# Retention in a two-block forward pass: plain products split into halves, squares summed on the Pool, wider value weights

## The chip, the core and the metric

The kernel runs on one core of one Trainium2 chip. The metric is the device time of one execution in microseconds, lower is better. One launch computes a whole forward pass over 512 tokens of width 1024 through several mixers and feed-forward layers, all of it in 32-bit floats.

## What is computed

The change touches one mixer, the retention of the second block ("odd"). Cut from the reference:

```python
def retention(q, k, v):                    # 4 heads, dk = 256, dv = 512
    ...
    dmask = jnp.where(diff >= 0, jnp.exp(lg[:, None, None] * jnp.maximum(diff, 0.0)), 0.0)
    ...
    def step(state, inp):
        qi, ki, vi = inp
        a = jnp.einsum('bhjd,bhmd->bhjm', qi, ki) * dmask
        o = jnp.einsum('bhjm,bhme->bhje', a, vi) + jnp.einsum('bhjd,bhde->bhje', qi, state) * xi
        state = state * g_chunk + jnp.einsum('bhmd,bhme->bhde', ki * zeta, vi)
        return state, o

def odd_mixer(h, w_in, out_norm, w_out, pos):
    z = h @ w_in
    q = rope(z[..., :nq].reshape(B, S, RET_HEADS, RET_QK), pos)
    k = rope(z[..., nq:2 * nq].reshape(B, S, RET_HEADS, RET_QK), pos)
    v = z[..., 2 * nq:2 * nq + nv].reshape(B, S, RET_HEADS, RET_V)
    g = z[..., 2 * nq + nv:]
    o = rmsnorm(retention(q, k, v), out_norm)
    o = o.reshape(B, S, nv).astype(h.dtype) * jax.nn.silu(g)
    return o @ w_out
```

## The kernel before

**Layout.** Activations lie transposed: 128 features in the partitions, 512 tokens along the row. The kernel needs no chunks: for each head it forms all causal scores of 512 x 512 tokens in four row blocks `j` of 128 key tokens, and block `j` needs only the queries from `j * 128` on, so its rows are 512, 384, 256 and 128 columns wide. `dec` holds the decay by distance.

**Products of halves.** A float product with a weight is made of three products on rounded halves. A value is split in `hi`, the value rounded to the type fp32r, and `lo`, the residual `value - hi`, which is rounded to fp32r too. `mm3` then adds `hi*hi`, `lo*hi` and `hi*lo` in one PSUM bank. ScalarE makes `hi` (a copy), VectorE makes `lo` (a subtraction). Some products are left plain: both operands are ordinary floats in `arena`, and the trace shows two MATMUL records for each of them. In the rows, `split` is the same memory as `arena`, seen as fp32r.

**Weights.** SyncE loads units of 2048 columns (1 MB) in turn into three buffers `wraw`; `W.round(act, name)` makes `whi` and `W.rest(dve, name)` makes `wlo`, in two buffers each. Both calls go up to one unit ahead of the unit named, and a unit's `whi` can't be written before TensorE is done with the unit two places earlier. So in the order of a head, the unit behind the one in use gets ready while that one is multiplied, provided that ScalarE and VectorE come to it in time. TensorE waits for a unit with `W.ready(name)`, which is VectorE's event.

**Order within a head** (`tensor` of `odd`): queries and keys (`u_qk`, two units of 256 columns, 4 blocks of 24 products of 512 columns, `x` moving); values (`u_v`, two units of 256 columns of weights, 8 blocks of 24 products of 256 columns, the weights moving beside 128 tokens of `x`); scores (8 plain products); gates (`u_g`, as queries); weighted values `o` (4 blocks of 4 plain products), with the squares of the block before summed by a plain product with `ones` (`sum_squares`) in between; then the output projection of the head before (`outs[hd - 1]`, 8 blocks of 12 products). The last head's projection follows at the end. `fm_tensor`, `tm_tensor` and `add_tensor` issue these blocks. Each engine runs its own list in the order written, and waits on counters of the others.

**Beside it.** ScalarE copies queries, keys and values out of PSUM (`raw`, `vt`), applies Silu to the gates, squares `o`, and after the fourth sum makes the root (table load, Ln, Exp: `rstd_scalar`) and the `hi` of the gated values. VectorE rotates queries and keys (12 operations into `qk`, waiting for the copy of all four blocks), multiplies the scores by `dec` into `pts`, and after the root gates each of four tiles (`stt` and `tt`), forms `lo` and, in between, adds the projection of the head before to the residual stream `h`. The gating of head `hd` so stands behind its own `o`, while TensorE does the projection of head `hd - 1`. The Pool fetches `dec` for each head and is otherwise free in this stage.

Of the kernel before, what the change touches and what calls it, by code (L numbers as in the profile page):

```python
# [11 lines left out]
P = 128  # L12
# [373 lines left out]
def build(nc, D, phases):  # L386
    ctx = ExitStack()
    with ctx:
# [2669 lines left out]
        def odd(ends, prev, nxt):  # L3058

            S = Stage("retention", sem)  # L3060
# [4 lines left out]
            raw = al(2048)  # L3065
            oo = [[als() for _ in range(4)] for _ in range(2)]
            cos, cos_src, l_c = con("cosq", "odd")
            sin, sin_src, l_s = con("sinq", "odd")
            qk, vt, pts, gg = (al(2048) for _ in range(4))
            tmp, rs, ot = al(T), al(T), [al(T), al(T)]  # L3070
            dec = al(512)
            l_dec = landing("dec")
            u_qk = [fm_units(f"qk{hd}", 512, [(Wi[:, hd * 256:hd * 256 + 256], 0), (Wi[:, 1024 + hd * 256:1280 + hd * 256], 256)])
                    for hd in range(4)]
            u_v = [tm_units(f"v{hd}", Wi, 2048 + hd * 512, 512, 4) for hd in range(4)]
# [3 lines left out]
            def tensor(pe):  # L3079
                for hd in range(4):  # L3080
                    for _ in fm_tensor(pe, S, u_qk[hd], X8, norm.made, fresh=None if hd else norm):
                        pass
                    for _ in tm_tensor(pe, S, u_v[hd], X8, norm.made):
                        pass
                    for j in range(4):
                        nt = T - j * P
                        b = ps.take("s", hd, j)
                        pe.wait_ge(S.V.of("roped", hd), ps.empty("s", hd, j))
                        for d in range(2):
                            i_ = pe.mm(b[:, 0:nt], qk[:, (2 + d) * T + j * P:(2 + d) * T + (j + 1) * P],  # L3090
                                       qk[:, d * T + j * P:(d + 1) * T], d == 0, d == 1)
                        i_.then_inc(*up(S.P, "s", hd, j))
                    for _ in fm_tensor(pe, S, u_g[hd], X8, norm.made):
                        pass
                    bss = ps.take("sum", hd)

                    def sum_squares(d):
                        pe.wait_ge(S.A.of("square", hd, d))
                        if d == 0:
                            pe.wait_ge(ps.empty("sum", hd))  # L3100
                        pe.mm(bss, ones, ot[d % 2], d == 0, d == 3).then_inc(*up(S.P, "sum", hd, d))

                    for d in range(4):
                        bo = ps.take("o", hd, d)
                        pe.wait_ge(S.V.of("pts", hd), S.A.of(f"v{hd}", 3, 1), ps.empty("o", hd, d))
                        for j in range(4):
                            i_ = pe.mm(bo[:, j * P:T], vt[:, j * 512 + d * P:j * 512 + (d + 1) * P],
                                       pts[:, j * T:j * T + T - j * P], j == 0, j == 3)
                        i_.then_inc(*up(S.P, "o", hd, d))
                        if d:  # L3110
                            sum_squares(d - 1)
                    sum_squares(3)
                    if hd:
                        for _ in add_tensor(pe, S, outs[hd - 1], oo[(hd - 1) % 2], [P] * 4, lambda k: S.V.of("o", hd - 1, k)):
                            pass
                for _ in add_tensor(pe, S, outs[3], oo[1], [P] * 4, lambda k: S.V.of("o", 3, k)):
                    pass

            def vector(dve):
# [7 lines left out]
                dve.wait_ge(l_c.of("x"), l_s.of("x"))  # L3127
                for hd in range(4):
                    for name, _, _, _ in u_qk[hd]:
                        W.rest(dve, name)  # L3130
                    for o in (0, 2):
# [302 lines left out]
```

## Time and profile before

| | us |
|---|---|
| median of 3 runs | 3285.48 (3285.32 to 3285.83) |
| the profiled execution | 3284.78 |
| its span in the trace | 3283.0 |
| TensorE busy (products) | 3114.7, 95% of the span |
| VectorE busy | 1558.8, 47% |
| ScalarE busy | 1175.8, 36% |
| Pool busy | 126.5, 4% |

The span runs from the first to the last instruction in the trace; the rest of the execution lies around it. The retention stage runs from about 2485 to 2909 us. The page gives busy times over the whole span; what a change in one stage is worth is read from the stage's own stretch: which engine is never idle there, who waits for whom, and how long the steps are that an engine has to do between two events. In a row of the timeline the first number is the start, the second the duration; products overlap, so what one costs is the distance from start to start.

### The profile page before, as it was taken

The numbers are of one execution on the slowest core, as the hardware profiler recorded it, in microseconds if no ns is written. First come the engines' busy times: TensorE is split into PE (matmuls) and PEld (weight loads), VectorE is DVE, ScalarE is ACT, GpSimd is POOL, SyncE is SP. The second block draws the span as 40 slices with busy tenths as digits, with TensorE's granted clock in tenths as the row PEclk, the third lists the DMA queues.
The fourth block names the chain that finished last, engine by engine and source line by source line (L and its number), as shares of the span: only waits on it lengthen the run. The fifth ranks groups of instructions, "written<-read, shape, count | busy, mean of one in ns | idle before, by whom it ended". The sixth has DMA issues, their size and how long they took to land.

```text
span 3283.0 us, 39941 instructions
## 1 busy us (share of the span) xinstructions
PE 3114.7 (95%) x17208; PEld 2490.4 (76%) x17208; DVE 1558.8 (47%) x1957; ACT 1175.8 (36%) x1564; POOL 126.5 (4%) x142
## 2 busy tenths in 40 slices
PE   8889988799999989899999998899999999999999
PEld 6787766577887766777887785588888887878887
DVE  4444446546544664546544654543335343363333
ACT  4343332434322464344322544532224322342221
POOL 1010000100000100100000200000001000000000
PEclk9899999899999999999999999999999999999999
DMA  4333001213332321313332231033323212133321
GB/s 150 119 131 104 15 21 40 77 52 90 103 90 85 94 64 52 103 42 97 92 97 78 91 90 52 26 94 98 93 87 116 81 64 93 65 103 90 103 90 64
DMA packets 355617, 270.60 MB, mean 82 GB/s; under 512 B 28672, under 2 KB 341504, under 8 KB 355184
## 3 DMA queue, kind: packets, MB, share of 16 engines
q1 hardware_dynamic: 351504, 252.83, 25.8%
q0 software_dynamic: 3936, 15.22, 1.3%
q8 instruction: 135, 2.21, 0.3%
q14 instruction: 42, 0.34, 0.0%
HBM read 261.73 MB, written 6.29 MB: 82 GB/s over the span
## 4 chain that ended last, share of the span: by engine, by line
PE 84%; DVE 8%; ACT 5%; issue 1%; POOL 0%; DMA 0%; DVEq 0%; SPq 0%; ACTq 0%; POOLq 0%
PE ps L189 83%; ACT arena L203 2%; DVE arena L220 2%; ACT whi L206 1%; DVE arena L212 1%; DVE wlo L212 1%; PE ps L192 1%; DVE hT L212 1%; DVE sml L229 1%; DVE xlo L220 1%; DVE arena L216 1%; ACT arena L206 0%; DVE split L212 0%; ACT L203 0%; POOL arena L212 0%
## 5 line engine op out<-in xcount | busy, mean ns | idle before, releaser
L189 PE MATMUL ps<-xhi,whi 128*128 128x512 f32 (+2 forms) x2192 | 874.1, 399 | 12.3 <-DVE wlo L212 4.2
L189 PE MATMUL ps<-xhi,wlo 128*128 128x512 f32 (+2 forms) x2192 | 857.1, 391 | 0.0
L189 PE MATMUL ps<-xlo,whi 128*128 128x512 f32 (+2 forms) x2192 | 856.7, 391 | 0.0
L189 PE MATMUL ps<-split,whi 128*128 128x512 f32 (+2 forms) x2640 | 830.9, 392 | 14.7 <-DVE split L212 10.4
L212 DVE TENSOR_TENSOR wlo<-wraw,whi 128x2048 fp32r<-128x2048 f32 (+4 forms) x258 | 550.7, 2137 | 475.6 <-ACT whi L206 475.4
L189 PEld LDWEIGHTS ps<-split,whi 128*128 128x128 f32 (+1 forms) x2640 | 491.5, 189 | 143.1 <-issue 26.6
L206 ACT ACTIVATE whi<-wraw 128x2048 fp32r<-128x2048 f32 (+4 forms) x258 | 456.2, 1771 | 352.8 <-PE ps L189 342.9
L189 PE MATMUL ps<-split,wlo 128*128 128x512 f32 (+2 forms) x1320 | 509.8, 386 | 0.0
L189 PEld LDWEIGHTS ps<-xhi,whi 128*128 128x128 f32 (+2 forms) x2192 | 410.9, 187 | 119.1 <-issue 10.4
L189 PEld LDWEIGHTS ps<-xhi,wlo 128*128 128x128 f32 (+2 forms) x2192 | 410.5, 187 | 91.9 <-issue 5.9
L189 PEld LDWEIGHTS ps<-xlo,whi 128*128 128x128 f32 (+2 forms) x2192 | 410.3, 187 | 90.6
L189 PE MATMUL ps<-arena 64*64 64x64 f32 (+8 forms) x4502 | 365.8, 268 | 47.9 <-DVE arena L212 28.5
L189 PEld LDWEIGHTS ps<-arena 64*64 64x64 f32 (+4 forms) x4502 | 272.4, 152 | 139.9 <-issue 54.6
L206 ACT ACTIVATE arena<-ps 128x512 f32<-128x512 f32 (+1 forms) x320 | 161.6, 517 | 544.8 <-PE ps L189 470.3
L212 DVE TENSOR_TENSOR arena<-arena,ps 128x512 f32<-128x512 f32 (+5 forms) x162 | 104.9, 648 | 414.6 <-PE ps L189 406.0
L212 DVE TENSOR_TENSOR hT<-hT,ps 128x512 f32<-128x512 f32 x216 | 148.4, 687 | 318.8 <-PE ps L189 312.4
L189 PEld LDWEIGHTS ps<-split,wlo 128*128 128x128 f32 (+1 forms) x1320 | 250.3, 190 | 54.4 <-issue 4.0
L206 ACT ACTIVATE split<-arena 128x512 fp32r<-128x512 f32 (+1 forms) x137 | 84.8, 619 | 424.6 <-DVE arena L212 412.8
L212 POOL TENSOR_TENSOR arena<-arena 128x512 f32<-128x512 f32 x66 | 91.1, 1385 | 2306.2 <-ACT arena L203 2305.3
L203 ACT ACTIVATE arena<-ps 128x512 f32<-128x512 f32 (+4 forms) x133 | 76.8, 583 | 260.3 <-PE ps L189 256.6
L203 ACT ACTIVATE arena<-arena 128x512 f32<-128x512 f32 (+4 forms) x161 | 94.9, 605 | 152.4 <-DVE arena L220 114.9
L212 DVE TENSOR_TENSOR split<-arena,split 128x512 fp32r<-128x512 f32 (+1 forms) x137 | 92.6, 676 | 89.9 <-ACT split L206 89.7
(110 smaller groups left out, 2041.3 us busy)
## 6 DMA issues: line engine op xcount, KB each, us to landing
wraw<-in_ffn_w_up SPq DMA_DIRECT2D x128, 512.0 KB, 5.2
wraw<-in_ffn_w_down SPq DMA_DIRECT2D x32, 1024.0 KB, 5.0
wraw<-in_odd_w_in SPq DMA_DIRECT2D x24, 1024.0 KB, 5.2
wraw<-in_ffn_w_gate SPq DMA_DIRECT2D x44, 512.0 KB, 3.9
wraw<-in_xattn_wkv SPq DMA_DIRECT2D x16, 1024.0 KB, 5.6
wraw<-in_xattn_wq SPq DMA_DIRECT2D x8, 1024.0 KB, 5.1
wraw<-in_xattn_wo SPq DMA_DIRECT2D x8, 1024.0 KB, 5.2
wraw<-in_cd_w_in SPq DMA_DIRECT2D x8, 1024.0 KB, 5.6
```

The lines of the kernel that those rows point to most:

```text
L189: return self.e.matmul(out, lhsT, rhs, start=start, stop=stop, skip_group_check=True)
L192: return self.e.transpose(out, in_, ident)
L203: return self.e.activation(out, in_, f, bias=bias, scale=scale, accum_out=acc)
L206: return self.e.activation(out, in_, ACT.Copy, scale=scale)
L212: return self.e.tensor_tensor(out, a, b, op)
L216: return self.e.tensor_scalar(out, a, s1, None, op0)
L220: return self.e.scalar_tensor_tensor(out=out, in0=a, scalar=s, in1=b, op0=op0, op1=op1)
L229: return self.e.tensor_reduce(out, a, AXX, ALU.max)
```

## The change

Only the retention stage (`odd`) is changed.

- **Scores and weighted values** become three products of halves each. Queries and keys are split after the rotation into `qk_hi` (ScalarE) and `qk_lo` (VectorE), values into `vh` and `vl`, weighted scores into `pts_hi` and `pts_lo`. The widths stay 512, 384, 256 and 128.
- **Values** come from two units of 512 columns that hold one half of the features each; the four token blocks stay open in four banks over both units. The number of products falls from 192 to 96 a head, at 512 columns instead of 256.
- **Squares**: the Pool adds the four squared tiles into `acc`, and one product with `ones` a head (`head_sum`) makes the sum.
- **Order**: the sum, root and gating of head `hd` move into head `hd + 1`: the sum behind the first query unit, root and `hi` copies on ScalarE between the query copies, the gating (`gates`) on VectorE in front of the rotation. The projection of heads 0 and 1 moves in front of the weighted values of the next head; that of head 2 stands behind the weighted values of head 3, with the last sum in its middle and the last gating beside it.
- The rotation is two steps (`turn`), the first of which needs only two of the four query blocks. Banks are handed out from fixed groups (`of=`).

```diff
@@ tensor
-                    for _ in tm_tensor(pe, S, u_v[hd], X8, norm.made):
-                        pass
+                    queries = fm_tensor(pe, S, u_qk[hd], X8, norm.made, of=(5, 6, 7) if hd else range(8), fresh=None if hd else norm)
+                    next(queries)
+                    next(queries)
+                    if hd:
+                        head_sum(hd - 1)
+                    run(queries)
+                    bs = [ps.take("v", hd, i, of=(4, 5, 6, 7)) for i in range(4)]
+                    for n, (name, parts, bn) in enumerate(u_v[hd]):
+                        u = W.take(name, parts, bn)
+                        for i in range(4):
+                            c = slice(i * P, (i + 1) * P)
+                            pe.wait_ge(W.ready(name), ps.empty("v", hd, i))
+                            for k in range(4):
...
-                            i_ = pe.mm(b[:, 0:nt], qk[:, (2 + d) * T + j * P:(2 + d) * T + (j + 1) * P],
-                                       qk[:, d * T + j * P:(d + 1) * T], d == 0, d == 1)
+                            pe.mm(b[:, 0:nt], qk_hi[:, k], qk_hi[:, q], d == 0, False)
+                            pe.mm(b[:, 0:nt], qk_lo[:, k], qk_hi[:, q], False, False)
+                            i_ = pe.mm(b[:, 0:nt], qk_hi[:, k], qk_lo[:, q], False, d == 1)
...
-                            i_ = pe.mm(bo[:, j * P:T], vt[:, j * 512 + d * P:j * 512 + (d + 1) * P],
-                                       pts[:, j * T:j * T + T - j * P], j == 0, j == 3)
+                            pe.mm(b[:, j * P:T], vh[:, v], pts_hi[:, p], j == 0, False)
+                            pe.mm(b[:, j * P:T], vl[:, v], pts_hi[:, p], False, False)
+                            i_ = pe.mm(b[:, j * P:T], vh[:, v], pts_lo[:, p], False, j == 3)
...
+                last = out_of(2, (5, 6, 7))
+                for _ in range(4):
+                    next(last)
+                head_sum(3)
+                run(last)
+                run(out_of(3, range(8)))
@@ vector
+                    if hd:
+                        for _ in gates(hd - 1):
+                            pass
+                    turn(hd, 0)
+                    turn(hd, 2)
+                    for n in range(4):
+                        t = slice(n * T, (n + 1) * T)
+                        dve.wait_ge(S.A.of("qk_hi", hd, n), S.V.own())
+                        dve.tt(qk_lo[:, t], qk[:, t], qk_hi[:, t].bitcast(F32), ALU.subtract).then_inc(*up(S.V, "qk_lo", hd, n))
+                    for name, _, _ in u_v[hd]:
                         W.rest(dve, name)
@@ gpsimd
+                    for d in range(1, 4):
+                        pool.wait_ge(S.A.of("square", hd, d), S.P.of("sum", hd - 1) if hd and d == 1 else NEVER, S.G.own())
+                        pool.tt(acc, sq[0] if d == 1 else acc, sq[d % 2], ALU.add).then_inc(*up(S.G, "added", hd, d))
```

On VectorE, between the weighted scores of head 0 and those of head 1, the list before reads as follows. The three rows from SCALAR_TENSOR_TENSOR on gate one tile, and come four times; the `wlo` row behind them is the unit of the first value weights, `x12` is the rotation, the next two `wlo` are the second value weights and the first gate weights.

```order
L220 SCALAR_TENSOR_TENSOR arena<-ps,par,arena 128x512
L212 TENSOR_TENSOR arena<-arena 128x512
L212 TENSOR_TENSOR split<-arena,split 128x512
L212 TENSOR_TENSOR wlo<-wraw,whi 128x2048
L212 TENSOR_TENSOR arena<-arena 128x512 x12
L212 TENSOR_TENSOR wlo<-wraw,whi 128x2048 x2
L212 TENSOR_TENSOR arena<-arena,ps 128x512
```

The changed list at the same place (the first value weights are the last of `x4`):

```order
L212 TENSOR_TENSOR wlo<-wraw,whi 128x2048 x4
...
L220 SCALAR_TENSOR_TENSOR arena<-ps,par,arena 128x512
L212 TENSOR_TENSOR arena<-arena 128x512
L212 TENSOR_TENSOR split<-arena,split 128x512 x2
L212 TENSOR_TENSOR arena<-arena 128x512 x12
L212 TENSOR_TENSOR split<-arena,split 128x512 x4
L212 TENSOR_TENSOR wlo<-wraw,whi 128x2048 x2
L212 TENSOR_TENSOR split<-ps,split 128x512 x4
L212 TENSOR_TENSOR arena<-arena,ps 128x512
```

The residual of the first value weights now stands in front of the gating, and that of the second value weights behind gating, rotation and four new residuals of queries and keys.

On TensorE, the end of head 0's values and its scores before:

```order
L189 MATMUL ps<-whi,xlo 128x256
L189 MATMUL ps<-arena 128x512 [waits retention_done_scalar,retention_done_vector]
L189 MATMUL ps<-arena 128x512
L189 MATMUL ps<-arena 128x384 [waits retention_done_scalar]
L189 MATMUL ps<-arena 128x384
L189 MATMUL ps<-arena 128x256 [waits retention_done_scalar]
L189 MATMUL ps<-arena 128x256
L189 MATMUL ps<-arena 128x128 [waits retention_done_scalar]
L189 MATMUL ps<-arena 128x128
```

and in the changed program:

```order
L189 MATMUL ps<-whi,xlo 128x512
L189 MATMUL ps<-split 128x512 [waits retention_done_vector]
L189 MATMUL ps<-split 128x512 x5
L189 MATMUL ps<-split 128x384 x6
L189 MATMUL ps<-split 128x256 x6
L189 MATMUL ps<-split 128x128 x6
```

Eight plain products became 24 products of halves, six of them 128 columns wide.

## Rows read from the trace of the kernel before

**Rows 1.** The page: busy time of each engine, share of the span, instructions.

```profile
PE 3114.7 (95%) x17208; PEld 2490.4 (76%) x17208; DVE 1558.8 (47%) x1957; ACT 1175.8 (36%) x1564; POOL 126.5 (4%) x142
```

**Rows 2.** The retention stage: stretch, length, busy of PE, PEld, DVE, ACT, POOL; clock.

```profile
2487.00:2909.00 422.00, 421.04 (x2138) 345.06 (x2137) 183.75 (x200) 138.38 (x168) 9.06 (x10) 1.00 0.26 84
```

**Rows 3.** Timeline of TensorE, head 0: start, duration, what; scores, then weighted values.

```profile
2531.12 4.48 PE L189 MATMUL ps<-arena 128*128 128x512 f32 x16
...
2535.66 0.39 PE L189 MATMUL ps<-xhi,wlo 128*128 128x512 f32 x1
...
2562.41 2.32 PE L189 MATMUL ps<-arena 128*128 128x512 f32 x8
2564.56 1.02 PE L189 MATMUL ps<-arena,ones 128*128 128x512 f32 x2
2565.42 2.32 PE L189 MATMUL ps<-arena 128*128 128x512 f32 x8
```

**Rows 4.** Timeline of ScalarE: copies behind two value blocks, and behind two gate blocks.

```profile
2528.44 0.38 ACT L206 ACTIVATE arena<-ps 128x256 f32<-128x256 f32 x1 [2.50 <-PE ps L189]
2531.32 0.38 ACT L206 ACTIVATE arena<-ps 128x256 f32<-128x256 f32 x1 [2.50 <-PE ps L189]
...
2541.10 0.60 ACT L203 ACTIVATE arena<-ps 128x512 f32<-128x512 f32 x1 [6.31 <-PE ps L189]
2546.54 0.60 ACT L203 ACTIVATE arena<-ps 128x512 f32<-128x512 f32 x1 [4.84 <-PE ps L189]
```

**Rows 5.** Timeline of TensorE, output projection: two products, three starts apart.

```profile
2662.54 0.39 PE L189 MATMUL ps<-split,wlo 128*128 128x512 f32 x1
...
2663.24 0.40 PE L189 MATMUL ps<-split,wlo 128*128 128x512 f32 x1
```

**Rows 6.** Timeline of TensorE in another stage: eight one-column products, and what follows.

```profile
1972.69 0.95 PE L189 MATMUL ps<-ones,arena 96*128 96x1 f32 x8
...
1973.82 0.39 PE L189 MATMUL ps<-split,wlo 128*128 128x512 f32 x1
```

**Rows 7.** Timeline of ScalarE: a copy, the next after a rounding between; a table load.

```profile
2557.43 0.60 ACT L203 ACTIVATE arena<-ps 128x512 f32<-128x512 f32 x1 [4.85 <-PE ps L189]
...
2559.72 0.59 ACT L203 ACTIVATE arena<-ps 128x512 f32<-128x512 f32 x1
...
2569.58 1.28 ACT L197 ACT_TABLE_LOAD   x1 [1.21 <-PE ps L189]
```

**Rows 8.** Timeline of VectorE: gating of one tile, then rotation and a weight residual.

```profile
2572.26 0.75 DVE L220 SCALAR_TENSOR_TENSOR arena<-ps,par,arena 128x512 f32<-128x512 f32 x1 [10.11 <-ACT arena L203]
...
2574.44 0.69 DVE L212 TENSOR_TENSOR split<-arena,split 128x512 fp32r<-128x512 f32 x1 [0.70 <-ACT split L206]
2575.17 0.75 DVE L220 SCALAR_TENSOR_TENSOR arena<-ps,par,arena 128x512 f32<-128x512 f32 x1
...
2697.54 8.19 DVE L212 TENSOR_TENSOR arena<-arena 128x512 f32<-128x512 f32 x12 [6.79 <-ACT arena L206]
2705.65 2.28 DVE L212 TENSOR_TENSOR wlo<-wraw,whi 128x2048 fp32r<-128x2048 f32 x1
```

**Rows 9.** Timeline of the Pool: one addition of squares at the stage's end.

```profile
2894.04 1.29 POOL L212 TENSOR_TENSOR arena<-arena 128x512 f32<-128x512 f32 x1 [168.66 <-ACT arena L203]
```

**Rows 10.** Timeline of TensorE in other stages: products behind long idle times (in brackets).

```profile
427.92 4.49 PE L189 MATMUL ps<-arena 128*128 128x512 f32 x34 [3.33 <-ACT arena L203]
...
438.67 4.69 PE L189 MATMUL ps<-arena 64*64 64x64 f32 x80 [3.50 <-DVE arena L212]
...
2016.73 2.43 PE L189 MATMUL ps<-xl,xf 128*128 128x128 f32 x8 [3.29 <-DVE xl L220]
```

**Rows 11.** Busy time by stretch, as rows 2: the clock behind those idle times.

```profile
429.00:431.00 2.00, 2.00 (x12) 1.07 (x12) 0.00 (x0) 0.97 (x1) 0.00 (x0) 0.50 0.00 0
...
444.00:446.00 2.00, 2.00 (x11) 1.48 (x9) 1.89 (x4) 0.00 (x0) 0.00 (x0) 0.83 0.00 0
...
2016.00:2018.00 2.00, 1.27 (x6) 1.09 (x7) 0.91 (x3) 0.59 (x2) 0.00 (x0) 1.00 0.00 0
```

## Prediction of the time, and its working

> **What bounds the kernel now.** I read the page first: TensorE is busy for 3114.7 us, 95% of the span, twice as long as the next engine [rows 1]. Then the retention stage alone, which is all that the change touches. From 2487 to 2909 TensorE is busy in 421.0 of 422.0 us at clock 1.00, VectorE in 183.8 and ScalarE in 138.4 [rows 2]. So every product taken from TensorE shortens the stage, until VectorE or ScalarE hands something over too late. The question is what is left after that "until". The profiled execution took 3284.78 us, 0.70 under the median of 3285.48; the sum is made against that execution, whose stages before and after this one stay as they are.
>
> **What TensorE saves.** Prices are start-to-start times, since a row's duration overlaps the next one.
> Values: a block of 24 products of 256 columns takes 2.88 us, from copy to copy [rows 4], 0.120 each. 768 of them are 92.2 us. Afterwards there are 384 of 512 columns. Products of 512 columns that move x cost 5.44 us per 24, 0.2267 each [rows 4]; those that move the arena cost 0.70 us per three, 0.233 each [rows 5]. No row moves weights of 512 columns beside x, so 0.2267 to 0.233. I take the first, because at 256 columns weights moved at the price x would: 87.1 us, a gain of 5.2. The other end gives 2.7.
> Squares: each product with `ones` takes 0.86 us (2564.56 to 2565.42) [rows 3]. Sixteen become four, a gain of 12 x 0.86 = 10.3. The additions move to the Pool, three per head of 1.29 us [rows 9], beside 10.9 us of the next head's queries.
> Scores: from 2531.12 to 2535.43 (the row at 2535.66 less 0.23), 4.31 us a head [rows 3]. Weighted values: 2.15 us per block of four products (2562.41 to 2564.56) [rows 3], four blocks, 8.6 us a head. The new version has three products of halves for each plain one. At 512, 384 and 256 columns I price them 0.233, 0.173 and 0.120 (columns at the slope between 256 and 512, 0.0417 us per 100, on the two rows known). At 128 columns the trace has no product of halves at all. Below: the same slope down to 0.067. Above: a plain product costs 4.31 us per 2560 columns, so 0.215 at this size, and the halves at 512 cost 0.227, which I take as the upper end. Between them stand products of one single column, which have to load 128 columns of weights each and still take 0.90 us per eight (1972.69 to 1973.82, less 0.23 for the product between), 0.112 [rows 6]. I take 0.112, since that row has the same number of weight columns per product and is the nearest. One row of four widths is then 0.638 us. Scores: 6 x 0.638 = 3.83, gain 0.48 a head, 1.9 in all. Weighted values: 12 x 0.638 = 7.66, gain 0.94 a head, 3.8 in all.
> TensorE's work shrinks by 5.2 + 10.3 + 1.9 + 3.8 = 21.2 us.
> By the Trainium skill, page TensorE: Matmul & The Clock Gate, section Back-to-back issue gap, a stream of weight load and product of 128 columns goes at about 81 ns; with that for the 72 narrow products the gain would be 72 x 0.031 = 2.2 us larger. No run here shows it.
>
> **What it waits for afterwards.** The gating of a head (twelve VectorE operations) moves from behind its own weighted values, where the output projection of the previous head covered it, to the middle of the next head's queries. There it stands in front of that head's rotation, of the four new residuals of queries and keys, and of the residual of the second value weights. Those weights are needed one unit after the queries end.
> Count from the end of the first query unit, heads 1 to 3. ScalarE's copy starts 0.20 after the next product has started (2531.32 against 2531.12) [rows 3, 4]; copy and rounding of the first value weights take 2.29 [rows 7]; table load, root and exponential 2.68 until the first gating operation (2569.58 to 2572.26) [rows 7, 8]. That is 5.2. Then VectorE alone: twelve gating operations that each wait for the one before, at 0.73 (2574.44 to 2575.17) or a little less [rows 8], 8.65; the rotation 8.11 [rows 8]; four residuals at 0.72, 2.9; the residual of the weights 2.29 [rows 8]. Sum 27.1. TensorE meanwhile has the one product with `ones` (0.86), the second query unit and the first value unit, 48 products each of 0.2267, 10.9 each: 22.6. **It waits 4.5 us, three times.** Before, only the rotation (8.1) stood there, and nothing waited.
> Head 0 has no gating in front. Its first value unit needs a PSUM bank that the last query copy empties (0.20 and one copy of 0.60 [rows 4, 7], about 0.8), and its second value weights come after rotation and residuals, about 0.8 late.
> Last head: the sum follows four blocks of the projection of head 2, with four more blocks behind it (48 x 0.233 = 11.2). Root 2.9, twelve gating operations 8.65 and four additions to h between them at 0.72 make 14.4. TensorE waits 3.2.
> Waits: 13.5 + 1.7 + 3.2 = 18.4, with 0.1 for each of some eight restarts 19.2. **Net of the work: 19.2 - 21.2 = -2.0 us.**
>
> **The clock.** Before, nothing in this stretch idles for long. Elsewhere in this trace TensorE idled 3.33 and 3.50 us, and each time the granted clock then stood at 0.50, half of 2.4 GHz, for a while: until 431, and into the stretch from 444 to 446, whose mean of 0.83 puts the end at 444.7 [rows 10, 11]. The price is half of that time: (431 - 427.9)/2 = 1.5 and (444.7 - 438.7)/2 = 3.0. Once, after 3.29 us, it stayed at 1.00 [rows 10, 11]. A wait of 4.5 us, which the view will show as some 4.3 idle, is longer than any of these. I take three falls at the mean of the two, 2.3 us, 6.9; the ends are 0 and 9.0. Nothing hides it, since TensorE is the bound.
> Sum: -2.0 + 6.9 = +4.9 us on 3284.78, 3289.7; the median of before lies 0.7 above that execution. I say 3290.
>
> **Rivals.**
> 1. The narrow products cost as much as the wide ones or as a plain product, 0.227. Nothing in the trace shows a product of halves under 256 columns at any price, so the rows can't refuse it. 72 x (0.227 - 0.112) = 8.3 more: +13.2 with the clock (3298.0), +6.3 without (3291.1). It decides for slower once a narrow product costs more than 0.13 with the clock fallen: +4.9 + 72 x 0.02 = +6.3.
> 2. The narrow products run at the pace of their columns, 0.067: 3.2 us less. With the clock +1.7, without -5.2 (3286.5 and 3279.6). For it: the slope between 256 and 512 is exact. Against it: the one-column products.
> 3. The waits don't come, because the second value weights get ready in the shadow of the first. Then the full 21.2 show: 3263.6. Against it stands the order on VectorE, where 27.1 us of work must fit in 22.6, each part from a row. It would need VectorE steps a sixth shorter.
> 4. The change doesn't shorten the products at all (three of halves as long as one plain one): that is rival 1 for all widths and contradicts three times 0.233 against 0.86 for 512 columns [rows 3, 5]. No chance of its own.
>
> **How the numbers follow.** The forecast's own case reaches from -2.0 (no fall of the clock) to +9.5 (three long falls, 9.0, and weights moved at 0.233, 2.5), 3283 to 3294; chance 0.42. Rival 1: 0.33. Rival 2: 0.15. Rival 3: 0.10. A measurement of this kernel can tell about 0.2%, 6.6 us, from no change. Faster by more: rival 3, 0.10. Slower by more: rival 1 nearly whole (0.32) and the upper end of the forecast's case (0.08), 0.40. Within: the rest, 0.50. Leaving out rival 3 and the last tenth of rival 1, the range is 3280 to 3300.
>
> **What would show it.** In the changed trace: value products of 512 columns every 0.227 us (right) or more; products of 128 columns in the scores every 0.112 (forecast), 0.067 or 0.227 us; scores of one head in 3.8 us and weighted values in 7.7; TensorE idle for VectorE's weight residual three times, each in the middle of a head's values, at about 4.3 us, and for the split residual after the last head about 3; a granted clock of 0.50 behind the three. If the idle times are under 2 us, the chain on VectorE was over-priced. If the clock stays at 1.00 behind them, the time is near 3283. If the time is under 3278, both the waits and the clock were wrong.

## The result, and the profile after

The changed kernel takes 3294.14 us (median of 13 runs, 3290.74 to 3297.84), the kernel before, measured beside it, 3285.83 us (13 runs, 3283.25 to 3291.50). The ratio is 1.0021 with a 95% interval of 1.0013 to 1.0029: slower by 4 to 10 us. The profiled execution took 3290.74 us, 5.96 more than the one of before (3284.78). The forecast for it was +4.9.

The page's row of busy time in the changed kernel (busy us, share of the span, instructions), which answers to [rows 1]:

```profile
PE 3101.4 (94%) x16896; PEld 2481.2 (75%) x16896; DVE 1587.0 (48%) x2005; ACT 1189.3 (36%) x1580; POOL 141.7 (4%) x154
```

TensorE is busy for 13.3 us less than before, and the program is slower. The stage shows why. Busy time per engine in the same stretch as [rows 2] (columns: us, busy time of each engine with its instructions, granted TensorE clock, DMA share, GB/s), and behind it the four places at which the clock fell:

```profile
2487.00:2909.00 422.00, 402.74 (x1801) 331.24 (x1800) 206.53 (x241) 149.17 (x178) 22.14 (x21) 0.98 0.25 81
2604.00:2608.00 4.00, 3.89 (x10) 3.12 (x11) 2.26 (x2) 0.00 (x0) 0.00 (x0) 0.57 0.64 214
2711.00:2718.00 7.00, 7.00 (x19) 5.51 (x20) 2.74 (x2) 0.60 (x1) 0.00 (x0) 0.60 0.86 300
2819.00:2824.00 5.00, 5.00 (x16) 3.91 (x17) 1.96 (x1) 0.54 (x1) 0.00 (x0) 0.66 0.75 270
2890.00:2894.00 4.00, 3.69 (x10) 2.75 (x11) 3.50 (x6) 2.29 (x2) 0.00 (x0) 0.59 0.00 0
```

TensorE was busy in 421.0 of 422.0 us before; now it stands still for 19.3, at a mean clock of 0.98 instead of 1.00. What a fall costs is the stretch times the missing share of the clock: 4 x 0.43 = 1.7, 7 x 0.40 = 2.8, 5 x 0.34 = 1.7, 4 x 0.41 = 1.6, together 7.8 us.

TensorE's timeline of the changed kernel, the products in front of which it waited, and between them the product with `ones` of head 0's sum, from which the chain is counted (start, duration, what it is; in brackets the idle time and who ended it):

```profile
2502.70 0.50 PE L189 MATMUL ps<-xhi,whi 128*128 128x512 f32 x1 [0.95 <-DVE xlo L212]
2509.28 0.47 PE L189 MATMUL ps<-whi,xhi 128*128 128x512 f32 x1 [0.78 <-ACT arena L206]
2521.25 0.50 PE L189 MATMUL ps<-whi,xhi 128*128 128x512 f32 x1 [0.81 <-DVE wlo L212]
...
2576.46 1.02 PE L189 MATMUL ps<-arena,ones 128*128 128x512 f32 x2
...
2598.89 0.39 PE L189 MATMUL ps<-whi,xlo 128*128 128x512 f32 x1
2604.11 0.79 PE L189 MATMUL ps<-whi,xhi 128*128 128x512 f32 x1 [4.83 <-DVE wlo L212]
...
2605.13 0.63 PE L189 MATMUL ps<-whi,xlo 128*128 128x512 f32 x1
2605.56 0.63 PE L189 MATMUL ps<-whi,xhi 128*128 128x512 f32 x1
...
2710.90 0.80 PE L189 MATMUL ps<-whi,xhi 128*128 128x512 f32 x1 [4.83 <-DVE wlo L212]
2818.82 0.62 PE L189 MATMUL ps<-whi,xhi 128*128 128x512 f32 x1 [4.83 <-DVE wlo L212]
2890.31 0.47 PE L189 MATMUL ps<-split,whi 128*128 128x512 f32 x1 [2.23 <-DVE hT L212]
2932.90 0.50 PE L189 MATMUL ps<-xhi,whi 128*128 128x512 f32 x1 [0.22 <-DVE xlo L212]
```

Three times, in the middle of a head's values, TensorE waits for the residual of weights (`wlo`): 5.22 us from start to start (2598.89 to 2604.11), where a product takes 0.23, so 4.99 are lost. Behind it the products come every 0.43 us (2605.13, 2605.56) instead of every 0.227: the low clock. At the end it waits 2.23 us; what releases it is one of VectorE's additions to `h` (`hT`).

The first and the last row of that fence are also the stage's two marks: the stage's first products with its new `x` (0.95 idle ahead, for `xlo`), and the same form at the head of the next stage. Between them the kernel before took 424.5 us (2502.41 to 2926.90), the changed one 430.2. This length comes from one profiled execution of each kernel. The experiments are read from it, since the program ahead of the mark, which no variant touches, ends between 2500.9 and 2506.1 from one profiled execution to the next.

VectorE's timeline at the first wait, the chain of the forecast; the two rows behind it are ScalarE's first copy and the last step of the root:

```profile
2581.76 0.75 DVE L220 SCALAR_TENSOR_TENSOR arena<-ps,par,arena 128x512 f32<-128x512 f32 x1 [0.37 <-ACT arena L203]
...
2590.41 8.26 DVE L212 TENSOR_TENSOR arena<-arena 128x512 f32<-128x512 f32 x12
2598.78 1.49 DVE L212 TENSOR_TENSOR split<-arena,split 128x512 fp32r<-128x512 f32 x2
2601.77 4.49 DVE L212 TENSOR_TENSOR wlo<-wraw,whi 128x2048 fp32r<-128x2048 f32 x2
```

```profile
2576.66 0.60 ACT L206 ACTIVATE arena<-ps 128x512 f32<-128x512 f32 x1 [4.84 <-PE ps L189]
2581.09 0.63 ACT L203 ACTIVATE arena<-arena 128x512 f32<-128x512 f32 x1
```

From start to start: up to the gating 5.30 (TensorE's product with `ones` starts at 2576.46, the first gating operation at 2581.76), gating 8.65 (to 2590.41), rotation 8.37 (to 2598.78), residuals of queries and keys 2.99 (to 2601.77), the weights' residual 2.3; TensorE goes on at 2604.11. Sum 27.65, forecast 27.1. VectorE has no idle time between its steps from the gating on.

### The profile page after: what moved, and what is told of

Same layout as the page of the kernel before. It is cut to its first block, busy times and chain, and to the rows that moved or that the text cites. A ratio compares the mean times of both kernels' runs of the same rounds, so it can differ in the third digit from the quotient of the medians.

```text
span 3289.0 us, 39432 instructions
## 1 busy us (share of the span) xinstructions
PE 3101.4 (94%) x16896; PEld 2481.2 (75%) x16896; DVE 1587.0 (48%) x2005; ACT 1189.3 (36%) x1580; POOL 141.7 (4%) x154
## 4 chain that ended last, share of the span: by engine, by line
PE 81%; DVE 11%; ACT 6%; issue 2%; POOL 0%; DMA 0%; DVEq 0%; SPq 0%; ACTq 0%; POOLq 0%
PE ps L189 80%; DVE arena L212 3%; ACT arena L203 2%; DVE arena L220 2%; ACT whi L206 2%; DVE wlo L212 2%; DVE split L212 1%; PE ps L192 1%; DVE hT L212 1%; DVE sml L229 1%; DVE xlo L220 1%; DVE arena L216 1%; ACT arena L206 0%; ACT L203 0%; POOL arena L212 0%
## 5 line engine op out<-in xcount | busy, mean ns | idle before, releaser
L189 PE MATMUL ps<-arena 64*64 64x64 f32 (+8 forms) x4310 | 313.8, 262 | 48.4 <-DVE arena L212 28.4
L189 PEld LDWEIGHTS ps<-arena 64*64 64x64 f32 (+5 forms) x4310 | 240.1, 151 | 117.7 <-issue 39.5
L206 ACT ACTIVATE arena<-ps 128x512 f32<-128x512 f32 (+2 forms) x288 | 149.2, 531 | 466.2 <-PE ps L189 392.7
L206 ACT ACTIVATE split<-arena 128x512 fp32r<-128x512 f32 (+1 forms) x169 | 101.6, 606 | 429.5 <-DVE arena L212 417.2
L212 POOL TENSOR_TENSOR arena<-arena 128x512 f32<-128x512 f32 x78 | 106.6, 1370 | 2533.6 <-ACT arena L203 2532.7
L212 DVE TENSOR_TENSOR split<-arena,split 128x512 fp32r<-128x512 f32 (+1 forms) x169 | 110.4, 659 | 80.8 <-ACT split L206 78.4
```

The costliest lines, as they stand in the source:

```text
L189: return self.e.matmul(out, lhsT, rhs, start=start, stop=stop, skip_group_check=True)
L206: return self.e.activation(out, in_, ACT.Copy, scale=scale)
L212: return self.e.tensor_tensor(out, a, b, op)
```

## The experiments

All times are compared with the kernel before, run beside them on the same chip; "stage" is the length between the two marks in the profiled execution. The theory: three measured gains on TensorE (values, squares, halves; 21 us) against waits for one chain on VectorE (some 18 us) and the clock that falls behind them (some 8 us). The rivals: narrow products cost as much as wide ones; the waits could not be removed; the clock costs nothing.

**The earlier residual.** One line on VectorE. `W.rest` goes one unit ahead of the unit that it names, so this line makes the residual of the second value weights.

```diff
                     turn(hd, 0)
+                    W.rest(dve, u_v[hd][0][0])
                     turn(hd, 2)
```

> The changed kernel with one line more: VectorE makes the residual of a head's second value weights between the two halves of the rotation instead of behind the rotation and the four residuals of queries and keys. Nothing is left out. Theory (TensorE's work fell by 21, its waits for that residual cost three times 4.99 us, and the clock that falls behind each costs 1.7, 2.9 and 1.7 more): the three waits go, and the 0.8 in head 0, so 15.8 of waits and 6.3 of clock, 22 us less than the changed kernel, less about 1 us that the later residuals of queries and keys may bring: 21. Against the kernel before, over which the changed one lies 6.9 us, that is -14 us, a ratio of 0.9957. No granted clock of 0.50 is left in heads 1 to 3. Rival 1, another wait takes its place (the scores then wait for the residuals of queries and keys, which are 2.3 us later): the waits move to the start of the scores and the ratio stays at 1.001 to 1.002. Rival 2, the waits cost what they last and the clock nothing: -9 us, 0.9972.

Measured: 3268.0 us (3266.37 to 3270.11), ratio 0.9945 [0.9933, 0.9958], stage 407.6 (2500.86 to 2908.50), 22.6 less than the changed kernel. VectorE's timeline in head 1 of this run, and TensorE's busy time and clock around head 2's values and at the end:

```profile
2587.43 4.08 DVE L212 TENSOR_TENSOR arena<-arena 128x512 f32<-128x512 f32 x6
2591.43 2.29 DVE L212 TENSOR_TENSOR wlo<-wraw,whi 128x2048 fp32r<-128x2048 f32 x1
2593.63 4.07 DVE L212 TENSOR_TENSOR arena<-arena 128x512 f32<-128x512 f32 x6
2597.80 3.08 DVE L212 TENSOR_TENSOR split<-arena,split 128x512 fp32r<-128x512 f32 x4
```

```profile
2690.00:2700.00 10.00, 10.00 (x46) 8.29 (x45) 9.52 (x13) 3.32 (x5) 0.00 (x0) 1.00 0.31 105
2866.00:2872.00 6.00, 5.10 (x20) 3.59 (x21) 5.35 (x6) 2.43 (x2) 0.00 (x0) 1.00 0.01 3
```

The residual is ready at 2593.7, 2.4 us before TensorE's first value unit ends (at 2596.1), and the ones of queries and keys, now 2.2 us later, are in time too: TensorE has no idle time left in heads 1 to 3. No wait took the place of the three in heads 1 to 3. The same 2.23 us of idle stand at the end, at 2866.09, but this time the clock stayed at 1.00: 1.7 us of the 22.6 are that. The rest, 20.9, is the three waits (3 x 4.99 = 15.0) and the one of 0.8 in head 0, less 0.8 for two waits of 0.4 that are new at the end, and by difference 5.9 of clock in heads 1 to 3.

**The wait filled.** 20 products ahead of the wait; they stand for it, and nobody reads their result.

```diff
+                            if hd:
+                                pe.wait_ge(S.V.of("gated", hd - 1, 3))
+                                for _ in range(20):
+                                    pe.mm(ps.aps[0], X8[0].hi[:, 0:P], X8[1].hi, True, True)
```

> The changed kernel with 20 products of 512 columns more on TensorE in each of heads 1 to 3, put where it waits for the residual of the second value weights. They read x, write a bank that nobody reads, and stand for the wait: 20 x 0.2267 = 4.5 us against 4.99 from start to start. The result needs nothing of them. Theory (the fall of the clock is a cost of its own, 6.3 us in heads 1 to 3): the wait stays as long as it was but the clock stays at 1.00 in heads 1 to 3, so 6.3 us less than the changed kernel, +0.6 us against before, a ratio of 1.0002. Rival (the clock's fall costs nothing, since the work that runs at the low clock is hidden, or it falls for another reason than the idle time): the ratio stays at 1.0021.

Measured: 3285.04 us (11 runs, 3282.70 to 3286.80), ratio 0.9995 [0.9987, 1.0004], stage 424.4 (2503.86 to 2928.28), 5.8 less than the changed kernel. Its timeline around head 1's wait, and the stretches behind it and at the end:

```profile
2600.07 0.39 PE L189 MATMUL ps<-whi,xlo 128*128 128x512 f32 x1
2600.29 4.69 PE L189 MATMUL ps<-xhi 128*128 128x512 f32 x20
2605.28 0.50 PE L189 MATMUL ps<-whi,xhi 128*128 128x512 f32 x1 [0.30 <-DVE wlo L212]
```

```profile
2604.00:2609.00 5.00, 4.70 (x21) 3.55 (x20) 3.43 (x2) 0.60 (x1) 0.00 (x0) 1.00 0.47 161
2885.00:2891.00 6.00, 5.34 (x17) 4.32 (x17) 5.33 (x7) 2.43 (x2) 0.00 (x0) 0.72 0.00 0
```

60 products more, TensorE goes on no earlier (4.99 us are still between the two units), and the stage is 5.8 us shorter, the median 9.1: what these products gave back is the clock. It stands at 1.00 behind all three, and falls only behind the unfilled wait at the end (6 x 0.28 = 1.7). So the price of the three falls, 6.2 by the rows above and 5.8 by this run, is real and comes on top of the waits. The rival (clock costs nothing, 1.0021) is out.

**The end reordered,** with the earlier residual and then alone.

```diff
-                for _ in range(4):
+                for _ in range(2):
...
+                gate_high(3, 0)
+                gate_high(3, 1)
                 W.round(act, outs[2][1][0])
-                for d in range(4):
-                    gate_high(3, d)
+                gate_high(3, 2)
+                gate_high(3, 3)
```

The first part stands twice, where TensorE places the last head's sum among the blocks of the projection of head 2, and where VectorE places the gating among the additions to h.

> As the kernel with the earlier residual, and beside it the end of the stage is reordered: the last head's sum comes after two blocks of the projection of head 2 instead of four, VectorE adds two blocks to h ahead of the gating instead of four, and ScalarE splits the first two gated halves before it rounds the last weights. Nothing is left out. Theory: the wait of 2.23 us at 2890.31 and the fall of the clock behind it (about 1.7) go, some 4 us less than with the earlier residual alone: -18 us against before, a ratio of 0.9945. Rival (the end is bound by VectorE's twelve gating operations whatever the order): the wait moves to the next sum or the first addition, and the ratio is that of the kernel with the earlier residual alone.

> The changed kernel with the reordered end alone: the last head's sum after two blocks of the projection of head 2, two blocks added to h ahead of the gating, the first two gated halves split before the last weights are rounded. The three waits for the residual stay. Nothing is left out. Theory: the wait of 2.23 us at the end shrinks to about 0.5 and the clock doesn't fall there, 1.7 + 1.7 us less than the changed kernel's stage of 430.2: 426.8 us. Rival: that fall belongs to the stage's pattern and not to this wait, then 428.5 us.

Measured with the earlier residual: 3265.93 us (3263.59 to 3270.07), ratio 0.9940 [0.9926, 0.9953], stage 404.6 (2503.93 to 2908.51). Alone: 3290.12 us (3287.58 to 3293.51), ratio 1.0011 [1.0001, 1.0020], stage 426.8 (2503.64 to 2930.47). TensorE's wait at the end in the second, and the clock around it:

```profile
2889.44 0.47 PE L189 MATMUL ps<-split,whi 128*128 128x512 f32 x1 [0.50 <-DVE hT L212]
```

```profile
2889.00:2895.00 6.00, 5.56 (x24) 4.57 (x25) 3.87 (x4) 3.00 (x3) 0.00 (x0) 1.00 0.12 27
```

Alone it gives 3.4 us (forecast 3.4: half wait, half clock). On top of the earlier residual it gives 3.0, though there the clock had not fallen: the wait shrinks by 1.7, and the two of 0.4 behind it go as well; the last 0.5 no run takes apart. The intervals of the two versions with the earlier residual overlap, so that only their stages tell them apart. early_end, 3265.93 us, is the fastest version here, some 20 us under the kernel before.

**Each gain by itself,** undone on the version that no longer waits. First the halves (their removal also from the changed kernel itself), then the sums, then the width of the value products:

```diff
-                            pe.mm(b[:, 0:nt], qk_hi[:, k], qk_hi[:, q], d == 0, False)
-                            pe.mm(b[:, 0:nt], qk_lo[:, k], qk_hi[:, q], False, False)
-                            i_ = pe.mm(b[:, 0:nt], qk_hi[:, k], qk_lo[:, q], False, d == 1)
+                            i_ = pe.mm(b[:, 0:nt], qk[:, k], qk[:, q], d == 0, d == 1)
```

and the same for the weighted values, without the copies and residuals that made the halves;

```diff
+                    for _ in range(3):
+                        pe.mm(b, ones, acc)
```

```diff
-                                pe.mm(bs[i], x.hi[:, c], u.hi[:, k, :], n == 0 and k == 0, False)
+                                for c0 in (0, 256):
+                                    w = slice(c0, c0 + 256)
+                                    pe.mm(bs[i][:, w], x.hi[:, c], u.hi[:, k, w], n == 0 and k == 0, False)
```

> The kernel with the earlier residual and the reordered end, and in it plain products for scores and weighted values. Nothing is left out. Here TensorE waits for nothing in heads 1 to 3, so the price of the halves stands alone. Theory: 4 x (4.31 - 3.81) + 4 x (8.60 - 7.62) = 5.9 us more than with halves, stage 404.6 + 5.9 = 410.5 us (up to 411.4 with some waiting at the end), 14 us under the kernel before, a ratio of 0.9957. Rival: the halves cost VectorE and ScalarE what they save TensorE, so nothing changes, 404.6 us.

> The kernel with the earlier residual and the reordered end, and in it four products with ones per head instead of one (three that are thrown away; the sum is the last one's). Nothing is left out. Theory: 12 x 0.86 = 10.3 us more, stage 414.9 us, a ratio to before of about 0.997. Rival: the sums were hidden and their removal gained nothing, 404.6 us, 0.994.

> The kernel with the earlier residual and the reordered end, and in it each value product of 512 columns cut into two of 256, as before. Nothing is left out. Theory: 768 x 0.120 instead of 384 x 0.2267, 5.1 us more, stage 409.7 us, a ratio of about 0.9955. Rival: with weights as the moving side 512 columns cost 0.233 like the arena's, 2.7 us more, 407.3 us.

> The changed kernel with its halves undone: scores and weighted values are plain products of float32, queries, keys, values and weights of the scores are not split, so eight residuals of VectorE and twelve copies of ScalarE per head are gone (four residuals of them, 2.9 us, stand in front of the one that TensorE waits for). Nothing of the computation is left out. Theory: TensorE's work grows by 4 x 0.50 for the scores and 4 x 1.0 for the weighted values, 6.0 us; each of the three waits shrinks by 2.9 from 4.99 us, 8.7 in all, and with 2.1 us left the clock doesn't fall behind them, 6.3 less. Stage from restart to restart 430.2 + 6.0 - 8.7 - 6.3 = 421.2 us, 3.3 under the kernel before, a ratio of 0.999. Rival 1, the clock falls all the same: 427.5 us, 1.0009. Rival 2, halves and plain products cost the same here and the gain came from elsewhere: 415.2 us, 0.9972.

Measured:

| kernel | time, us | ratio to before | stage, us | against its base |
|---|---|---|---|---|
| early_end (base) | 3265.93 | 0.9940 [0.9926, 0.9953] | 404.6 | |
| early_end_plain | 3276.32 | 0.9961 [0.9947, 0.9975] | 410.4 | +5.9 (expected 5.9) |
| early_end_sums | 3276.88 | 0.9970 [0.9958, 0.9981] | 414.8 | +10.3 (expected 10.3) |
| early_end_v256 | 3273.17 | 0.9954 [0.9939, 0.9969] | 409.7 | +5.1 (expected 5.1) |
| after (base) | 3294.14 | 1.0021 [1.0013, 1.0029] | 430.2 | |
| plain | 3284.12 | 0.9989 [0.9979, 0.9998] | 420.0 | -10.2 (expected -9.0) |

The stages add up: 404.6 with 5.9 + 10.3 + 5.1 = 21.3 more would be 425.9, the kernel before has 424.5, and the new version still waits 0.78 in head 0 and 0.51 at the end, which before doesn't. In early_end_v256 the two halves of a value tile share a bank of PSUM, and the kernel computes wrong values, which its expectation did not foresee; number and shape of the products are as stated. By the Trainium skill, page PSUM — Partial Sum Buffer, section PSUM: the matmul accumulator, the first product of a sum clears the marks of its whole bank. By that rule the first half's sum so far is lost when the second half begins; no run here tests this cause.

plain is the odd one: it undoes a gain and becomes faster than the changed kernel, and by 0.1% (0.02 to 0.21%) than the kernel before. Its three waits on the timeline read 1.63 us each, the first of them, with the clock behind it:

```profile
2603.67 0.50 PE L189 MATMUL ps<-whi,xhi 128*128 128x512 f32 x1 [1.63 <-DVE wlo L212]
```

```profile
2603.00:2609.00 6.00, 5.33 (x23) 4.41 (x24) 2.90 (x2) 1.64 (x2) 0.00 (x0) 1.00 0.68 222
```

The wait is 3.2 us shorter: 2.99 for the four residuals of queries and keys, and 0.2 because the rotation takes 8.17 here and not 8.37; why, no run shows. That makes 9.6 us for three heads, and the clock as well. So in the changed kernel the halves cost more than they save, and on the version without waits they save 5.9. That is the whole case in one pair of runs.

**The price of narrow products.** In head 0, in front of the last block of scores, 192 products of halves of six widths:

```diff
+                        if hd == 0 and j == 3:
+                            for w in (64, 128, 192, 256, 384, 512):
+                                for _ in range(32):
+                                    pe.mm(b[:, 0:w], qk_hi[:, 0:P], qk_lo[:, 0:w], True, True)
```

> The changed kernel with 192 products of halves more in head 0, 32 each of 64, 128, 192, 256, 384 and 512 moving columns, weights of 128 columns, all into a bank that the next product clears. The result needs nothing of them. It measures the price of a narrow product of halves by itself. By the forecast 0.112 us at 128 columns, 0.120 at 256, 0.173 at 384 and 0.233 at 512, so about 0.11 at 64 and 192 too if loading the 128 columns of weights sets a floor. Rival 1: 0.227 at every width. Rival 2: the columns alone set it, 0.033, 0.067 and 0.093 at 64, 128 and 192. From the scores of the changed kernel, 3.81 us a head, a price of 0.10 at 128 columns is worked out; this run must agree with it. The time grows by some 27 us.

One execution: 3323.15 us. The clock stood at 1.00 over the 64 columns, which came first, and fell to 0.50 behind them, so the prices of 128 and 192 columns are mixed:

```profile
2539.00:2548.00 9.00, 9.00 (x44) 9.00 (x44) 0.00 (x0) 0.00 (x0) 0.00 (x0) 0.50 0.00 0
```

Hence a second form, one width a head, on the version without waits:

```diff
+                        if j == 3:
+                            for w in ((64, 128, 192, 256)[hd],):
+                                for _ in range(100):
+                                    pe.mm(b[:, 0:w], qk_hi[:, 0:P], qk_lo[:, 0:w], True, True)
```

> The kernel with the earlier residual and the reordered end, and in each head, in front of the last block of the scores, 100 products of halves more: 64 columns wide in head 0, 128 in head 1, 192 in head 2 and 256 in head 3. The result needs nothing of them. In the run with the added products of six widths the granted clock stood at 0.50 for 10 us in the middle of narrow products, with no idle time of TensorE ahead of it. Theory 1 (narrow products by themselves bring the clock down): it falls to 0.50 in heads 0 and 1, perhaps 2, and not in head 3. Theory 2 (that fall came from the wait of 0.8 us in head 0 or from chance): it stays at 1.00 in heads 1 to 3. At clock 1.00 the start-to-start times are 0.112 at 64, 128 and 192 columns and 0.120 at 256; at 0.50 0.213 at 128.

One execution, 3321.07 us. TensorE's timeline: a head's scores with the 100 added products (24 + 100), and the product behind them, for heads 1 and 3; the view of busy times for heads 0 to 3:

```profile
2630.41 15.09 PE L189 MATMUL ps<-split 128*128 128x512 f32 x124
2645.34 0.44 PE L189 MATMUL ps<-xhi,whi 128*128 128x512 f32 x1
...
2852.96 15.92 PE L189 MATMUL ps<-split 128*128 128x512 f32 x124
2868.72 0.44 PE L189 MATMUL ps<-xhi,whi 128*128 128x512 f32 x1
```

```profile
2537.00:2542.00 5.00, 5.00 (x47) 5.00 (x46) 0.17 (x1) 0.57 (x2) 0.00 (x0) 1.00 0.01 3
2543.00:2559.00 16.00, 16.00 (x65) 14.94 (x65) 4.19 (x6) 3.39 (x3) 0.00 (x0) 0.50 0.00 0
2634.00:2645.00 11.00, 11.00 (x100) 11.00 (x100) 0.17 (x1) 0.57 (x2) 0.00 (x0) 1.00 0.01 1
2745.00:2755.00 10.00, 10.00 (x92) 10.00 (x92) 0.42 (x1) 0.84 (x2) 0.00 (x0) 1.00 0.01 2
2856.00:2867.00 11.00, 11.00 (x94) 11.00 (x93) 0.56 (x2) 0.94 (x2) 0.00 (x0) 1.00 0.00 0
```

Of each stretch 3.8 us are the head's own 24 products. Head 1 (128 columns): (2645.34 - 2630.41 - 3.8)/100 = 0.111 us. Head 2 (192 columns) has the same 15.09 us for its 124 products, so 0.111 too. Head 3 (256 columns): (15.76 - 3.8)/100 = 0.120. Head 0 (64 columns) shows about 0.11 too, as long as the clock was at 1.00 (47 products touch the 5.00 us). So from 64 to 192 columns a product of halves costs 0.111 whatever its width: rivals 1 (0.227) and 2 (0.067) are both out. The clock fell in head 0 alone. That is what the expectation's theory 2 says for heads 1 to 3, and of theory 1 it leaves at most the 64 columns. The two runs with 64 columns in head 0 show a fall there, and none of the other ten executions of the changed kernel and its variants does, though each has a wait of 0.78 us in that head. So neither that wait nor chance is likely; but 64 columns were tried in head 0 only, so width and place are not separated.

**The changed kernel once more.**

> The changed kernel once more, beside its variants. Expected as before: a ratio to the kernel before of 1.0021 (6.9 us), and a stage of 430.2 us from restart to restart. If its time on this chip differs, the differences of the variants are to be read from their stages and not from their medians.

Measured: 3293.24 us (3289.47 to 3297.55), ratio 1.0020 [1.0011, 1.0030], stage 430.3 (2506.05 to 2936.37), again with four falls of the clock. The stage repeats to 0.1 us in these two executions, while the mark at its head lies 3.4 us later than in the first execution.

## Where the prediction was right, and where not

**Work of TensorE: right.** Forecast 21.2, measured 21.3: values 5.1 (5.2, so weights of 512 columns moved at the price of `x`, 0.2267, not the arena's), sums 10.3 (10.3), halves 5.9 (5.7). The changed kernel's own rows agree (TensorE's timeline, head 0):

```profile
2532.27 3.92 PE L189 MATMUL ps<-split 128*128 128x512 f32 x24
...
2536.31 0.39 PE L189 MATMUL ps<-xhi,wlo 128*128 128x512 f32 x1
...
2557.88 7.78 PE L189 MATMUL ps<-split 128*128 128x512 f32 x48
2565.50 0.44 PE L189 MATMUL ps<-xhi,whi 128*128 128x512 f32 x1
```

Scores: 2536.31 - 0.23 - 2532.27 = 3.81 us (forecast 3.83); weighted values 7.62 (7.66). The choice that carried most of the risk was 0.112 for a product of 128 columns, taken from [rows 6]. Its number was right, and products of halves do have a price that doesn't depend on the width below 256 columns. That the one-column products are held by the same thing is not shown: they are plain, so the eight records of [rows 6] are four products with two records each, and the agreement to 0.001 may be in part luck. The ~81 ns that the Trainium skill, page TensorE: Matmul & The Clock Gate, section Back-to-back issue gap, gives for such a stream is over a fourth less than the 0.111 measured: the trace decides against it for products of halves.

**The waits: in heads 0 to 3 right in place and cause and, within 0.5 us, size.** Forecast three times 4.5 and 0.1 for the restart, a term for which no row stood; measured 4.99, which the view shows as 4.83 of idle time (forecast there: 4.3); the 0.16 between the two is the restart. What is missing is in the chain, 27.65 for 27.1: 0.1 at its head, 0.1 in the residuals, and 0.26 in the rotation, which took 8.37 and not 8.11; gating, 8.65, and TensorE's side, 22.66 against 22.6 (2576.46 to 2598.89 and one product), were met. Head 0's two waits, 0.78 and 0.81, as forecast.

The last head's wait was forecast at 3.2 and was 2.23, and here the chain was another than the forecast's. Two rows of VectorE in front of it:

```profile
2881.45 2.29 DVE L212 TENSOR_TENSOR wlo<-wraw,whi 128x2048 fp32r<-128x2048 f32 x1 [0.33 <-ACT whi L206]
...
2889.47 0.69 DVE L212 TENSOR_TENSOR hT<-hT,ps 128x512 f32<-128x512 f32 x1
```

The forecast put all twelve gating operations and four additions in front of TensorE's restart (11.5 us). TensorE went on at 2890.31, behind the addition that ends at 2890.16. From the start of the gating (2879.65) up to there stand eight gating operations, three additions and a residual of weights of 2.29 us that the forecast left out: 10.5 us. Two errors partly cancel; the size is near in part by luck.

Rival 3, that the waits don't come, was wrong for this kernel; one moved line makes it true.

**The clock: right that it falls three times, short by one.** Forecast 3 x 2.3 = 6.9, measured 1.7 + 2.8 + 1.7 = 6.2, and 1.6 more behind the last wait, of 2.23 us, for which no fall was counted. The term that was too small is this one, and the step behind it is the sentence by which only waits as long as those of [rows 10] were priced. Even its own figure for the last wait, 3.2 us, lay beside 3.29 without a fall and 3.33 with one. And the trace of the kernel before held shorter waits with a fall behind them (TensorE's timeline, then the clock in the stretches that follow):

```profile
2028.51 4.07 PE L189 MATMUL ps<-xl,xf 128*128 128x128 f32 x8 [2.02 <-ACT arena L203]
...
2051.13 3.49 PE L189 MATMUL ps<-xl,xf 128*128 128x128 f32 x8 [2.58 <-ACT arena L203]
```

```profile
2028.00:2032.00 4.00, 3.49 (x8) 2.28 (x8) 0.00 (x0) 4.00 (x8) 0.00 (x0) 0.57 0.00 0
2050.00:2056.00 6.00, 4.87 (x12) 2.16 (x13) 2.72 (x10) 4.55 (x12) 0.00 (x0) 0.72 0.17 45
```

In the same trace a wait of 2.49 us (ahead of 548.55) was followed by none. Filling the three waits showed the clock to be a cost of its own.

**The sum.** -21.3 of work, waits of 3 x 4.8 + 0.8 + 0.8 + 2.2 = 18.2, 7.8 of clock, and about 0.1 for each of some seven restarts: +5.4 for the stage, which the two marks give as 5.7. The profiled execution shows +5.96 on +4.9 forecast. The medians show 8.3 on 4.5; most of that distance lies outside the stage, where nothing is changed, in the few us by which executions of one kernel differ, so only the interval (4 to 10 us) is to be taken from them. The misses of single terms (+1.2 for the waits in heads 1 to 3, -1.0 at the end, +0.9 for the clock) partly cancel. The changed kernel's 3294.14 lies in the forecast range, 3280 to 3300, but the case "within 0.2%", given the largest chance, is just missed by the ratio, 1.0021, whose interval lies on both sides of that bound.

## What to carry to other kernels

When work is taken from the engine that bounds a stage, list what the next engines must finish between two of its hand-overs: here a chain of 27.65 us on ScalarE and VectorE stood where TensorE had 22.7, and 21 us of real savings turned into a loss. The cure was to look for the one hand-over that is due first (a 2.3 us residual) and to move it ahead of work that is due later, which took one line and gave 22.6 us. Work that is added to the engine with time to spare is not free at such a place: the halves cost more there than they saved. For small differences compare the length of the changed stage between two fixed marks, which repeated to 0.1 us in two executions, and not the medians, since single executions of one kernel spread over 7 to 8 us.

## What the runs showed of the hardware beyond that

- The granted clock fell to 0.50 with TensorE busy all the time: in the run with one width a head in the middle of the 100 products of 64 moving columns, at about 2542 (1.00 up to there, 0.50 from 2543 to 2559, longer than the stream, behind which wide products come from 2553.95 on), and in the other such run behind 32 of them. The same number of 128, 192 or 256 columns in heads 1 to 3 kept 1.00. The Trainium skill, page TensorE: Matmul & The Clock Gate, section HAM oscillation — how this bites in real kernels, names idle gaps as what bites; these rows have no idle time just ahead of the fall.
- A wait of 2.2 us at the same place (2.16 to 2.23) was followed by a fall in the changed kernel (both executions), in the one with filled waits, the one with plain products and the one with six widths, and by none in the one with the earlier residual: five of six. The waits of 4.83 us were all followed by one, twelve of twelve; three waits of 1.63 us by none. A wait of 2 to 3 us has to be priced with a chance, not with a bound.
- A product of halves costs 0.111 us at 128 and at 192 columns, about as much at 64, 0.120 at 256, 0.2267 at 512, with 128 columns of weights.
